# A merged output projection through memory, with seven half products for eight

## The reference, cut to what matters

```python
h = rmsnorm(x, pre_norm_w)                       # x: 2048 tokens x 1024
q, k, v, z_att, b, c, u, z_conv, g_att, g_conv = split(h @ w_in)
att  = rmsnorm(diff_attention(q, k, v)) * silu(z_att)      # 2048 x 512
conv = b * conv3(c * u) * silu(z_conv)                     # 2048 x 512
m = (sigmoid(g_att + bias0) * (att @ w_att_out)
     + sigmoid(g_conv + bias1) * (conv @ w_conv_out))      # 2048 x 1024
out = x + rmsnorm(m @ w_out, post_norm_w)                  # w_out: 1024 x 1024
```

## Time and profile before

| | |
|---|---|
| median of 3 runs | 1739.46 us (1738.71 to 1740.19) |
| the profiled execution's own time | 1740.0 us |
| its span in the profile | 1738.1 us (mean granted PE clock 0.999) |
| PE busy | 1701.3 us, 98% |
| DVE busy | 1087.6 us, 63% |
| ACT busy | 665.6 us, 38% |
| POOL busy | 272.3 us, 16% |

### The profile page before, as it was taken

One profiled execution on the slowest core, in us unless ns is written; L12 is line 12 of the kernel. 1 busy time (PEld: TensorE's weight loads), 2 busy tenths in 40 slices (PEclk: granted clock), 3 DMA queues, 4 the chain that ended last, 5 costly groups with the idle time before them and its releaser, 6 DMA issues.

```text
span 1738.1 us, 22885 instructions
## 1 busy us (share of the span) xinstructions
PE 1701.3 (98%) x8296; PEld 1418.6 (82%) x8296; DVE 1087.6 (63%) x2151; ACT 665.6 (38%) x1184; POOL 272.3 (16%) x194
## 2 busy tenths in 40 slices
PE   7999999999999999999999998999999899999998
PEld 6888888888788888888888887888888788888887
DVE  5538566645877877747777776777867453424242
ACT  5423233224333323215455454554555442323231
POOL 0000000265522332311110022111111040000000
PEclk9999999999999999999999999999999999999999
DMA  7447999754425433297677558856567865353532
GB/s 242 139 162 298 384 350 335 251 155 144 146 76 167 120 99 114 80 293 242 197 202 233 137 165 247 248 172 179 167 176 224 290 232 189 109 182 112 180 111 71
DMA packets 161886, 331.04 MB, mean 190 GB/s; under 512 B 15714, under 2 KB 60770, under 8 KB 156258
## 3 DMA queue, kind: packets, MB, share of 16 engines
q1 hardware_dynamic: 160610, 327.38, 59.4%
q10 hardware_dynamic: 1152, 2.10, 0.3%
HBM read 218.26 MB, written 111.16 MB: 190 GB/s over the span
## 4 chain that ended last, share of the span: by engine, by line
PE 87%; DVE 5%; DMA 3%; issue 2%; POOL 1%; ACT 1%; SPq 1%; DVEq 0%; ACTq 0%
PE bank L1245 14%; PE bank L1246 14%; PE bank L1247 14%; PE bank L1422 13%; PE bank L1327 5%; PE bank L1329 5%; PE bank L1330 5%; PE bank L1382 5%; PE bank L1354 3%; PE bank L1355 3%; PE bank L1365 3%; DVE e L2181 2%; DVE at_lo L2217 1%; PE bank L1255 1%; PE bank L1402 1%
## 5 line engine op out<-in xcount | busy, mean ns | idle before, releaser
L1327 PE MATMUL bank<-ht,a_op 128*128 128x512 f32 x504 | 196.3, 390 | 2.4 <-DVE stage L1958 1.2
L1330 PE MATMUL bank<-ht,a_op 128*128 128x512 f32 x504 | 196.1, 389 | 0.0
L1329 PE MATMUL bank<-ht,a_op 128*128 128x512 f32 x504 | 196.1, 389 | 0.0
L1720 ACT ACTIVATE e<-e,nbias 128x128 f32<-128x128 f32 (+15 forms) x128 | 153.6, 1200 | 80.7 <-DVE nbias L2190 80.6
L2181 DVE CUSTOM_DVE_ANT_0 e<-bank,zeros 128x512 f32<-128x512 f32 x192 | 124.9, 688 | 90.3 <-PE bank L1355 90.1
L1245 PE MATMUL bank<-ht,w 128*128 128x512 f32 x448 | 174.4, 389 | 0.0
L1246 PE MATMUL bank<-ht,w 128*128 128x512 f32 x448 | 174.3, 389 | 0.0
L1247 PE MATMUL bank<-ht,w 128*128 128x512 f32 x448 | 174.3, 389 | 0.0
L1422 PE MATMUL bank<-ht,w 128*128 128x512 f32 x624 | 168.7, 395 | 0.0
L1229 POOL TENSOR_SCALAR mask<-kc,qc 128x128 f32<-128x128 f32 (+3 forms) x64 | 87.7, 1370 | 495.8 <-DVE mx L2181 495.3
L1382 PE MATMUL bank<-at_hi,v_sl 128*128 128x256 f32 (+1 forms) x576 | 118.9, 285 | 14.7 <-DVE at_lo L2217 14.2
(11 more groups left out here) (188 smaller groups left out, 3515.7 us busy)
## 6 DMA issues: line engine op xcount, KB each, us to landing
w<-split_s SPq DMA_DIRECT2D x92, 512.0 KB, 4.8
raw<-in_w_in SPq DMA_DIRECT2D x64, 512.0 KB, 5.4
split_s<-piece SPq DMA_DIRECT2D x24, 1024.0 KB, 5.7
q_st<-qk_s SPq DMA_DIRECT2D x128, 128.0 KB, 4.9
ring<-gate_s SPq DMA_DIRECT2D x64, 256.0 KB, 3.4
ht_s<-ht SPq DMA_DIRECT2D x6, 2048.0 KB, 9.5
gate_s<-gate_st SPq DMA_DIRECT2D x48, 256.0 KB, 4.9
qk_s<-stage SPq DMA_DIRECT2D x48, 192.0 KB, 3.9
```

The lines of the kernel that those rows point to most:

```text
L1327: nc.tensor.matmul(out[:], hi, right[:, k, 0, :], start=k == 0 and not adds, stop=False, skip_group_check=adds)
L1329: nc.tensor.matmul(out[:], hi, right[:, k, 1, :], start=False, stop=False, skip_group_check=adds)
L1330: mm = nc.tensor.matmul(out[:], lo, right[:, k, 0, :], start=False, stop=k == 3, skip_group_check=adds)
L1720: nc.scalar.activation(e, e, ACT.Exp, bias=nbias[G % 2][:, h:h + 1], scale=SCALE, accum_out=esum[G % 2][:, h:h + 1]).then_inc(exp_done, 1)
```

## The change

The merge becomes two passes.

**First pass**: m of all four blocks, 64 products, `o = (2 * n + half) * KT + m`: all eight m of the attention branch, then all eight of the convolution branch. The gated attention half stays in `m_acc` (ten buffers), the convolution gate goes through `m_c` (three buffers), the sum is stored to memory (`m_s`), without a split. Branch weights are loaded in halves of 512 KB. `w_out` is loaded by two row tiles at a time from the second block on; POOL forms the differences T1 to T4, three of which go through memory (`t_s`); ACT and DVE split the four others in the same pass. Nothing of `w_out` is loaded during attention any more. The splits of T2, T3 and T4 come after the last product of the first pass.

**Second pass**: the 16 token tiles as 8 pairs, seven products of 12 matmuls each, in the order of `F_PRODUCTS`: the first two pairs are interleaved (P1, P2, P5, P6, P7, P4, P3, each for q = 0 and q = 1), then one pair after another (P1, P5, P6, P7, P2, P4, P3). m comes back from memory by pairs (1 MB). A half row lies in `f_bank(q, x, half)`; pair q uses the same four banks as pair q - 2. The row's two halves are needed for its norm, so both banks of a row are free only when `finish` has written the output.

```diff
+F_PRODUCTS = [(q, x) for x in FIRST_TWO for q in (0, 1)] + [(q, x) for q in range(2, F_PAIRS) for x in ONE_PAIR]
+ROWS = [(0, 1), (1, 1), (0, 0), (1, 0)] + [(q, x) for q in range(2, F_PAIRS) for x in (1, 0)]
+ROW_AT = {qx: i for i, qx in enumerate(ROWS)}
...
+        def f_bank(q, x, half):
+            return 4 * ((q + 1) % 2) + {(0, 0): 2, (0, 1): 3, (1, 0): 0, (1, 1): 1}[x, half]
...
         @block.sync
-                        if TILES - 6 <= R < TILES - 6 + WO_KEPT:
-                            load_wo(R - TILES + 6)
...
+            for n in range(NB):
...
+                sp.wait_ge(y_done, n * 2 * KT + KT)
+                if n < NB - 1:
+                    for i in range(KT // 2):
+                        load_branch(n + 1, i)
+                else:
+                    for x in range(2, 5):
+                        for j in range(2):
+                            sp.dma_start(t_raw[x, j][:], t_s[x - 2, j]).then_inc(t_loaded, 16)
+                for m in range(KT):
+                    store_m(n, m)
+                    if n * KT + m + C_RING < NB * KT:
+                        load_c(n * KT + m + C_RING)
...
         @block.tensor
             for n in range(NB):
-                for m in range(KT):
...
-                for o in range(2, 2 * QPB):
-                    rows(o, range(KT))
+                for half in range(2):
+                    for m in range(KT):
+                        o = (2 * n + half) * KT + m
...
+                        if o >= 4:
+                            pe.wait_ge(y_gated, o - 3)
+                        for k in range(4):
...
                         mm.then_inc(y_done, 1)
+            def row_product(i):
+                q, x = F_PRODUCTS[i]
+                base = 4 * ((q + 1) % 2)
+                pe.wait_ge(w_hi_done, f_split_at(i))
+                pe.wait_ge(w_lo_done, f_split_at(i))
+                if x == "P1":
+                    out, b = base + 2, 0
+                    if q >= 2:
+                        pe.wait_ge(f_out, 2 * ROW_AT[q - 2, 0] + 1)
...
+                elif x == "P3":
+                    out, b = base + 3, -2
+                    pe.wait_ge(sum_done, f_added(q, "C22"))
...
         @block.scalar
+            split_ft(2)
+            take_f1(0)
+            take_f1(1)
...
+            split_f(16)
+            split_f(17)
+            for q in (0, 1):
+                square(q, 1, 0)
+                root(q, 1)
+            split_f(18)
+            split_f(19)
+            for q in (0, 1):
+                square(q, 0, 1)
+                root(q, 0)
+            take_f1(2)
+            for q in range(2, F_PAIRS):
+                i = F_POS[q, ONE_PAIR[0]] + A_SLOTS
+                for j in range(4):
+                    split_f(i + j)
+                square(q, 1, 1)
+                split_f(i + 4)
+                square(q, 0, 0)
+                split_f(i + 5)
+                square(q, 1, 0)
+                root(q, 1)
+                split_f(i + 6)
+                square(q, 0, 1)
+                root(q, 0)
+                if q + 1 < F_PAIRS:
+                    take_f1(q + 1)
         @block.vector
+            def finish(q, x):
+                r = ROW_AT[q, x]
+                ss = y_ss[r % 4]
+                dve.wait_ge(f_root, r + 1)
+                nc.vector.reciprocal(ss[:, 2:3], ss[:, 3:4]).then_inc(f_recip, 1)
...
+                for half in range(2):
+                    dve.wait_ge(f_scaled, weighed_at[q, x, half])
+                    nc.vector.scalar_tensor_tensor(out=x_row(r)[:, half], in0=bank[f_bank(q, x, half)][:],
+                                                   scalar=ss[:, 2:3], in1=x_row(r)[:, half], op0=ALU.mult, op1=ALU.add
+                                                   ).then_inc(f_out, 1)
...
+            for q in (0, 1):
+                weigh(q, 1, 0)
+                add_up(q, 1)
+            split_f(18)
+            split_f(19)
+            for q in (0, 1):
+                finish(q, 1)
+            for q in (0, 1):
+                rows_c12(q)
+            for q in (0, 1):
+                weigh(q, 0, 1)
+                add_up(q, 0)
+            for q in (0, 1):
+                finish(q, 0)
+            for q in range(2, F_PAIRS):
+                i = F_POS[q, ONE_PAIR[0]] + A_SLOTS
+                split_f(i)
+                split_f(i + 1)
+                rows_u2(q)
+                split_f(i + 2)
+                split_f(i + 3)
+                rows_u3(q)
+                rows_c22(q)
+                weigh(q, 1, 1)
+                split_f(i + 4)
+                weigh(q, 0, 0)
+                rows_c21(q)
+                split_f(i + 5)
+                weigh(q, 1, 0)
+                add_up(q, 1)
+                finish(q, 1)
+                rows_c12(q)
+                split_f(i + 6)
+                weigh(q, 0, 1)
+                add_up(q, 0)
+                finish(q, 0)
```

More of the change, by code:

```diff
@@ L501, in late_wo_lo, with late_m, late_op @@
-        def late_wo_lo(k):
-            sub = ExitStack()
-            wo_raw[k] = held(f"wo_raw{k}", [P, D], F32, sub)
-            sub.close()
-            wo_lo[k] = held(f"wo_lo{k}", [P, D], F32R, late)
-        def late_ring(i):
-            ring[i] = held(f"ring{i}", [P, BLK], F32, late)
+        def late_m(i):
+            m_acc[i] = held(f"m_acc{i}", [P, BLK], F32, late)
+        f_op = []
+        def late_op():
+            f_op.append(held(f"f_op{len(f_op)}", [P, 2, BLK], F32R, late))
@@ L1124, in _ @@
-            for place, s_ in enumerate(y_stored):
-                sp.wait_ge(s_, 16 * rows_before(NB, (place - NB * USES) % RING))
+                    for i in range(KT // 2, KT):
+                        load_branch(n + 1, i)
+            for r in range(4):
+                load_row(r)
+            load_m(2)
+            load_m(3)
+            for r in range(NT):
+                q, x = ROWS[r]
+                if q >= 2 and x and q + 2 < F_PAIRS:
+                    load_m(q + 2)
+                store_row(r)
+                if 1 <= r <= NT - 4:
+                    load_row(r + 3)
@@ L1496, in _ @@
+            for i in range(len(F_PRODUCTS)):
+                row_product(i)
         @block.scalar
@@ new lines, in take_f1, with square @@
+            def take_f1(q):
+                act.wait_ge(proj_done, f_product_at(F_POS[q, "P1"]))
+                if q >= 2:
+                    act.wait_ge(sum_done, f_added(q - 2, "U2"))
+                else:
+                    act.wait_ge(m_stored[3], m_stores(3, NB))
+                nc.scalar.activation(f_p1[q % 2][:], bank[f_bank(q, 0, 0)][:], ACT.Copy).then_inc(p1_out, 1)
+            squared = 0
+            def square(q, x, half):
+                nonlocal squared
+                rows_formed(act, q, x, half)
+                if squared:
+                    act.wait_ge(f_sq, squared)
+                r = ROW_AT[q, x]
+                if r >= 4:
+                    act.wait_ge(f_recip, r - 3)
+                nc.scalar.activation(squares[:], bank[f_bank(q, x, half)][:], ACT.Square,
+                                     accum_out=y_ss[r % 4][:, half:half + 1]).then_inc(f_sq, 1)
+                squared += 1
@@ new lines, in root @@
+            def root(q, x):
+                r = ROW_AT[q, x]
+                act.wait_ge(f_sum, r + 1)
+                nc.scalar.activation(y_ss[r % 4][:, 3:4], y_ss[r % 4][:, 2:3], ACT.Sqrt, bias=eps[:],
+                                     scale=1.0 / D).then_inc(f_root, 1)
+            for o in range(4, NB * 2 * KT):
+                sigmoid(o)
+                if o // KT in (2, 3, 4, 5) and o % KT == 5:
+                    split_rows(o // KT - 2)
+                if o // KT == 2 * NB - 1 and o % KT in (3, 4, 6):
+                    for i in range(2):
+                        split_f(2 * (3, 4, 6).index(o % KT) + i)
@@ new lines, in gate @@
+            def gate(o):
+                half, m = o // KT % 2, o % KT
+                a = o // (2 * KT) * KT + m
+                dve.wait_ge(gate_ready, o + 1)
+                dve.wait_ge(y_done, o + 1)
+                acc, c = m_acc[a % M_RING][:], m_c[a % C_RING][:]
+                r = c if half else acc
+                nc.vector.tensor_tensor(r, bank[o % 4][:], r, ALU.mult).then_inc(y_gated, 1)
+                if half:
+                    dve.wait_ge(y_gated, o + 1)
+                    nc.vector.tensor_tensor(acc, acc, c, ALU.add).then_inc(m_sum, 1)
@@ new lines, in rows_u3 @@
+            def rows_u3(q):
+                dve.wait_ge(sum_done, f_added(q, "U2"))
+                dve.wait_ge(proj_done, f_product_at(F_POS[q, "P7"]))
+                if q >= 2:
+                    dve.wait_ge(sum_done, f_added(q - 2, "C21"))
+                else:
+                    dve.wait_ge(m_stored[0], m_stores(0, NB))
+                nc.vector.tensor_tensor(f_u3[q % 2][:], bank[f_bank(q, 1, 1)][:], f_u2[q % 2][:], ALU.add
+                                        ).then_inc(sum_done, 1)
@@ new lines, in _ @@
```

(13 more changed lines are left out.)

624 lines of the change are left out of this document (395 added, 229 removed).

## The result

The changed kernel takes 1756.01 us (median of 4 runs, 1755.10 to 1760.54), the kernel before in the same session 1739.09 us (4 runs, 1737.17 to 1740.19). The ratio is 1.0095 [1.0081, 1.0109]: **slower by some 17 us**, where 1729 was forecast. The profiled execution took 1755.4 us with a span of 1753.4, 15.3 above the span before. That is the difference to explain.

What follows compares the result with a forecast made beforehand. PE was taken as the bound (busy 1701.3 of 1738.1 us). -21.8 - 3.5 - 1.0 + 10.6 + 2.0 + 0.5 + 2.6 = -10.6 from 1740.0 gave 1729.4 profiled, 1729 us median; 1721 to 1738 held 8 in 10.

Steps and rivals of the forecast that it cites:

- Matmuls: Second pass: 672 matmuls in place of 768, 96 fewer at 0.2267 us of PE's time each; -21.8 us.
- I take -3.5: End of attention: without `w_out` loads the gate store lands earlier, ending PE's 2.1 us wait and the half speed; -3.5 us.
- close, 0 to 2 us; I take 0: Start of the first pass: 3.25 MB, 9.6 us of loading, arrive within 10.9 us of products; 0 us put.
- each load has a half pass of time: First pass: stores and loads lie beside PE, 2 MB of branch loads in each 21.8 us; no cost put.
- The fourth rival: First pass held up by convolution gates in three buffers, if landing takes 8 us; +2 to +8 us, chance 0.06.
- `wa`: -1.0: First pass: PE's wait of 1.0 us for `wa` goes, its loads no longer behind ring loads; -1.0 us.
- The opening: Second pass, before P1 of pair 2: PE waits for `finish(0, 0)`, behind other work in DVE's queue; +10.6 us.
- 2.0 put: After the wait at the second pass's opening: PE's clock at half; +2.0 us, bounds 1.6 and 2.7.
- Pairs paced by the loop (0.13): Pairs 3 to 7: PE waits for C22 as POOL's sums block DVE's splits, loop 22.2 us; 1742 us, chance 0.13.
- The tail: After the last matmul: C12 1.3 us late behind `finish(7, 1)`, root not hidden, 0.6; +2.6 us, bounds 1.4 and 4.

Runs made afterwards that it cites:

- experiment 8: experiment 4 with a 1 MB load of `wa` meant to go behind the last gate stores, but issued ahead of the awaited store; 1741.64 us, 0.9999.
- Experiments 7: experiment 4 without the attention branch loads for the second to fourth block (6 MB less); 1736.94 us, 0.9973.
- 12: experiment 4 without the loads of convolution gates after the first three (7.25 MB less); 1729.55 us, 0.9935.
- experiments 1: The changed kernel with the `w_out` rows ahead of the convolution branch loads in SP's queue; 1751.57 us, 1.0055.
- experiment 3: The changed kernel with the six T loads put two by two behind gate loads in the last half pass; 1752.37 us, 1.0060.
- Experiment 2: The changed kernel with the end of pair 0 written before that of pair 1 at the second pass's opening; 1746.12 us, 1.0026.
- experiments 10: experiment 4 with odd row tiles and T parts issued behind the fifth `m`, and T loads behind the last gate loads; 1734.58 us, 0.9959.
- 11: The kernel of experiments 10 with C12 and the sum of squares earlier on DVE in the last pair; 1732.81 us, 0.9961.
- experiment 9: experiment 4 with the branch loads of blocks 1 to 3 issued on POOL's queue instead of SP's; 1751.61 us, 1.0068.
- experiment 4: The changed kernel with the edits of experiments 1, Experiment 2 and experiment 3 together; 1738.18 us, 0.9981.

## Why the prediction was wrong, point by point

**Matmuls: right.** From 1628.51 us to the end of the last product at 1744.96 PE does six pairs in 116.45 us; 6 x 19.04 and 2.2 for the clock are 116.4. The price of 0.2267 us held.

**"I take -3.5" at the end of attention: wrong.** It named the `w_out` loads as what kept the gate store back, "two stand in the queue then". They did not: they were issued at 1343.85 and 1346.73 us, and none of the eight such loads took more than 10.8 us to land, so that both were in by 1357.5. The store was issued at 1363.88. Ahead of it in the queue stood other loads, of `wa`, `w` and the branch. With those of `w_out` gone, the DMA share is 0.06 from 1354 to 1356 us (0.74 before), but at 1360 to 1370 it is 1.02 again, the store takes 8.9 us, and the wait is 2.1 us, with 1.7 lost at half clock. In eleven of the experiments the wait is 1.5 to 2.3 us, and 5.0 in experiment 8, with 1 MB more ahead of the store. So bulk ahead of the store does lengthen the wait, but the bulk there was not that of `w_out`. Whether the wait ends with `wa` moved behind it was not run and stays open.

**The first pass, "close, 0 to 2 us; I take 0" and "each load has a half pass of time": this step failed.** It made +20.4 out of -1.0. The weighing was by bytes and by bandwidth, load for load, and each load alone does have its time. (Its sum for the first halves of `wa` was a little low as well: 3.25 MB at 337 GB/s are 10.1 us, if a MB is what it is in "1 MB or 3.1 us", and not 9.6.) It left out that SP's queue is in order and that a gate load in it waits for a sum of m. So the queue has a lead of no more than three gates. As the landing grows from 3.4 us to 5.7 (12.9 behind the T loads), this lead is used up, and everything behind a gate is late too. Experiments 7 and 12 tell the two apart: 6 MB of bulk out gave 1.4 us, 7.25 MB of gates out gave 8. The last half pass shows it directly: with 3 MB ahead of the gates, among them, and behind them, they land after 10.2, 7.7 and 4.3 us, and the wait at its end is 3.5, 2.7 and 0.6 us. How the 20.4 us divide is known only roughly, since the gains of experiments 1, 3 and 12 (7, 6 and 8 us) each carry some 4 us of doubt.

**The fourth rival was this mechanism, at a chance of 0.06 and a price of 2 to 8 us.** Its landing of 8 us lies between the median of 5.7 and the longest of 13.0. Two things were missing. What is late is not only the gate but rows and branches behind it, and ACT and DVE stand in order at the split of late rows, so that PE runs out of banks (7.6 us at once). And it had no clock: 6.0 us were lost at half clock.

**`wa`: -1.0, not certain.** No such wait is in the trace of the changed kernel, but ten of the twelve experiments, which load `wa` no later, show one of 1.7 to 2.9 us there.

**The opening: right in mechanism, 1.3 us too large.** DVE's timeline shows the queue as it was followed: splits 18 and 19, `finish` of rows (0, 1) and (1, 1), then, behind C12 of both pairs, `finish(0, 0)`:

```profile
1619.27 1.39 DVE L2581 TENSOR_TENSOR wa<-wo_rows,wa 128x512 fp32r<-128x512 f32 x2 [0.88 <-ACT wa L2029]
...
1620.77 1.41 DVE L2646 SCALAR_TENSOR_TENSOR t_raw<-bank,y_ss,t_raw 128x512 f32<-128x512 f32 x2
1622.28 1.41 DVE L2646 SCALAR_TENSOR_TENSOR t_raw<-bank,y_ss,t_raw 128x512 f32<-128x512 f32 x2
...
1627.61 1.41 DVE L2646 SCALAR_TENSOR_TENSOR t_raw<-bank,y_ss,t_raw 128x512 f32<-128x512 f32 x2
```

PE's timeline at its end, with durations of 0.63 us for 0.39 behind it, the granted clock at half:

```profile
1628.51 0.76 PE L1697 MATMUL bank<-f_op,wa 128*128 128x512 f32 x1 [9.30 <-DVE t_raw L2646]
1629.07 0.63 PE L1699 MATMUL bank<-f_op,wa 128*128 128x512 f32 x1
```

2.2 us were lost to it (2.0 put). Experiment 2 shows that the stall hung on the written order and not on the scheme.

**Pairs paced by the loop (0.13): did not happen.** PE has no wait after 1634 us. The splits of `w_out`'s sums in the first pass show the contention that this rival went by (lines of the kernel after, as in the earlier trace rows):

```profile
L2568 DVE TENSOR_TENSOR f_op<-wo_rows,f_op 128x512 fp32r<-128x512 f32 x12 | 15.2, 1320 | 16.6 <-ACT f_op L2006 16.6
L2581 DVE TENSOR_TENSOR wa<-wo_rows,wa 128x512 fp32r<-128x512 f32 x12 | 8.2, 685 | 0.9 <-ACT wa L2029 0.9
```

An operation of the same kind takes 1320 ns in the mean where most run beside POOL's differences (678 to 1782 for single ones), and 685 where POOL mostly rests (681 to 692). The Trainium skill's rule on the two locking each other out (SBUF — State Buffer, "Who interferes with whom") agrees. It did not set the time in the pairs, where PE never waited for it.

**The tail: right**, +2.8 for +2.6: C12 stood behind the two output halves of row (7, 1). DVE, timeline after:

```profile
1745.27 1.41 DVE L2646 SCALAR_TENSOR_TENSOR t_raw<-bank,y_ss,t_raw 128x512 f32<-128x512 f32 x2
1746.60 0.69 DVE L2618 TENSOR_TENSOR bank<-bank,m_acc 128x512 f32<-128x512 f32 x1
```

**The sign.** The saving of 21.8 us was real, and more than it was spent, in three places: 11.5 us on an order of work that could be written otherwise, 2.8 in the tail, and 20.4 in a pass that moves as many bytes as the whole merge before in 55% of the time. With the order mended (experiments 10 and 11) the scheme wins 7 us of its 21.8, known to some 2 us.

## What to carry to other kernels

When a change puts the same bytes into less time, don't ask only whether bandwidth suffices. Take each small load that sits on a short ring, price it at a landing under load (here 6 to 13 us in place of 3.4), and see what stands behind it in the same in-order queue and who stands still for that. Issue bulk behind urgent loads in one queue, and read in the trace whether an edit did that: here one edit put a load ahead of the store that it was to follow (experiment 8). A second queue was no way out (experiment 9). And where the first units of a new loop are interleaved, write the end of the first one ahead of the second's, since the first is what frees the bank.

## What the runs showed of the hardware that was not expected

- *Waits of the same length have different prices.* A wait of 1.8 us in experiment 4 (it ends at 1479.7 us) was followed by 1.7 us lost at half clock; one of 3.0 us at the end of the first pass in experiment 3 by none; one of 1.7 us at the opening of experiment 2 by none. The same program can go either way: the wait at the end of attention, 2.1 us in the changed kernel and 2.2 in experiment 2, cost 1.7 us there and nothing here. No rule for it came out of these runs.
- *Moving bulk loads to POOL's queue slowed the loads that stayed*: gates of 256 KB from 6.6 to 8.1 us, rows from 8.0 to 10.5 (experiment 9).
- *One load of 1 MB more ahead of a store of 256 KB made PE's wait for it 3.3 us longer*, 5.0 us for 1.7 (experiment 8; a gate's landing in the last half pass moved in the same way, from 10.2 to 4.3 us, when 3 MB went behind it).
